# Expert cells of a two-block layer: who makes the low parts of the finished output tiles

## The reference, cut to what matters

```
he = jax.nn.silu(t @ exp_w1[e]) * (t @ exp_w3[e])      # 1024 -> 256
y  = y + comb[:, e:e + 1] * (he @ exp_w2[e])           # 256 -> 1024
```

## Time and profile before

| | |
|---|---|
| time, median of 3 runs | 2053.93 us (2053.76 to 2054.52) |
| span of the profiled execution, first to last instruction | 2052.0 us |
| TensorE busy | 1980.4 us, 97% |
| VectorE busy | 1415.1 us, 69% |
| ScalarE busy | 968.7 us, 47% |
| GpSimd busy | 24.6 us, 1% |
| mean granted TensorE clock | 0.988 |

### The profile page before, as it was taken

How to read it: one execution, slowest core, us unless ns; L and a number is a source line. 1 busy time by engine, 2 the same in 40 slices (tenths; PEclk the granted TensorE clock), 3 DMA queues, 4 the chain that set the end, 5 groups by cost and what they waited for, 6 DMA issues and landing times.

```text
span 2052.0 us, 26626 instructions
## 1 busy us (share of the span) xinstructions
PE 1980.4 (97%) x8972; PEld 1565.2 (76%) x8972; DVE 1415.1 (69%) x2180; ACT 968.7 (47%) x1409; POOL 24.6 (1%) x46
## 2 busy tenths in 40 slices
PE   7999999989999999899999999999998999999997
PEld 7887888877776778666667888888875678888885
DVE  7985443557999775857756888873387578888533
ACT  5666333446777335366654433333365454333221
POOL 0000000001000000000000000000000000000000
PEclk9999999999999999999999999999999999999998
DMA  4220322327999145300002233333341033332332
GB/s 182 79 67 20 94 92 92 98 77 262 356 353 340 62 113 161 106 1 1 2 1 90 88 99 92 92 102 103 103 119 41 12 102 98 96 92 92 103 103 82
DMA packets 65418, 219.09 MB, mean 107 GB/s; under 512 B 9584, under 2 KB 10768, under 8 KB 65200
## 3 DMA queue, kind: packets, MB, share of 16 engines
q1 hardware_dynamic: 60192, 211.04, 31.6%
q10 hardware_dynamic: 5136, 6.89, 1.4%
HBM read 209.04 MB, written 2.10 MB: 103 GB/s over the span
## 4 chain that ended last, share of the span: by engine, by line
PE 80%; DVE 11%; ACT 3%; issue 3%; DMA 1%; ACTq 1%; SPq 0%; DVEq 0%
PE psum L946 56%; PE psum L1370 5%; PE psum L1541 3%; PE psum L1296 2%; PE psum L1343 1%; PE psum L1677 1%; DVE w_lo L2645 1%; PE psum L1524 1%; PE psum L1353 1%; PE psum L1522 1%; PE psum L1110 1%; DVE sig L2892 1%; PE psum L1477 1%; PE psum L1538 1%; ACTq L1898 1%
## 5 line engine op out<-in xcount | busy, mean ns | idle before, releaser
L946 PE MATMUL psum<-x_hi,w_hi 128*128 128x512 f32 (+1 forms) x1344 | 497.8, 381 | 2.5 <-DVE w_lo L2645 1.4
L946 PE MATMUL psum<-x_lo,w_hi 128*128 128x512 f32 (+1 forms) x1344 | 497.7, 381 | 0.0
L946 PE MATMUL psum<-x_hi,w_lo 128*128 128x512 f32 (+1 forms) x1344 | 495.2, 379 | 0.0
L2645 DVE TENSOR_TENSOR w_lo<-raw,w_hi 128x1024 fp32r<-128x1024 f32 x243 | 296.5, 1220 | 188.7 <-ACT w_hi L1783 188.2
L1783 ACT ACTIVATE w_hi<-raw 128x1024 fp32r<-128x1024 f32 x243 | 255.6, 1054 | 208.0 <-DMA raw<-stream 205.5
L946 PEld LDWEIGHTS psum<-x_hi,w_hi 128*128 128x128 f32 x1344 | 246.7, 188 | 58.0 <-DVE w_lo L2645 2.8
L946 PEld LDWEIGHTS psum<-x_lo,w_hi 128*128 128x128 f32 x1344 | 246.4, 188 | 51.6 <-issue 1.4
L946 PEld LDWEIGHTS psum<-x_hi,w_lo 128*128 128x128 f32 x1344 | 247.0, 188 | 49.7
L946 PE MATMUL psum<-hid_hi,w_hi 128*128 128x512 f32 (+1 forms) x688 | 259.7, 385 | 11.8 <-DVE w_lo L2645 11.3
L946 PE MATMUL psum<-hid_lo,w_hi 128*128 128x512 f32 (+1 forms) x688 | 258.6, 384 | 0.0
L946 PE MATMUL psum<-hid_hi,w_lo 128*128 128x512 f32 (+1 forms) x688 | 257.9, 383 | 0.0
(11 more groups left out here) (611 smaller groups left out, 2996.5 us busy)
## 6 DMA issues: line engine op xcount, KB each, us to landing
raw<-stream SPq DMA_DIRECT2D x251, 512.0 KB, 3.6
raw<-experts SPq DMA_DIRECT2D x70, 512.0 KB, 5.3
raw_more<-experts SPq DMA_DIRECT2D x68, 512.0 KB, 5.3
staged<-staged ACTq DMA_DIRECT2D x80, 64.0 KB, 3.2
resid<-x_fm SPq DMA_DIRECT2D x4, 528.0 KB, 6.9
out_fm<-resid SPq DMA_DIRECT2D x4, 512.0 KB, 2.9
consts<-consts_in SPq DMA_DIRECT2D x1, 1373.0 KB, 13.0
kv_pairs<-kv_even_odd ACTq DMA_DIRECT2D x4, 256.0 KB, 7.4
```

The costliest lines, as they stand in the source:

```text
L946: last = pe.matmul(o, wt[:, slot, k * P:(k + 1) * P], m[part], start=start and p == 0, stop=stop and p == 2, skip_group_check=True)
L2645: dve.tensor_tensor(w_lo[:, slot, :], raw[:, slot, :], w_hi[:, slot, :].bitcast(F32), ALU.subtract)\
```

## The change

The low part of tiles 0 to 5 of `Y` moves from VectorE's queue to GpSimd's. GpSimd issues the six subtractions after it has set `Y` to zero, each behind a wait for the high part. VectorE keeps those of tiles 6 and 7, and before that of tile 6 waits until the six others are done.

```diff
@@ gpsimd
             for k in range(TILES):
                 pool.memset(Y[:, k, :], 0.0).then_inc(y_zeroed, 1)
 
+            for k in range(TILES - 2):
+                pool.wait_ge(y_hi, k + 1)
+                pool.tensor_tensor(YL[:, k, :], Y[:, k, :], YH[:, k, :].bitcast(F32), ALU.subtract).then_inc(y_lo, 1)
+
             pool.wait_ge(lin_done, L0["scat"] + C)
@@ vector
             def output_lo(k):
 
                 dve.wait_ge(y_hi, k + 1)
+                if k == TILES - 2:
+
+                    dve.wait_ge(y_lo, k)
                 dve.tensor_tensor(YL[:, k, :], Y[:, k, :], YH[:, k, :].bitcast(F32), ALU.subtract).then_inc(y_lo, 1)
@@ vector, loop over the cells
                 hidden_gate(c)
                 if c:
                     moe_low(6 * c + 6)
-                if c >= N_EXP + 1:
-                    output_lo(c - N_EXP - 1)
```

## The result

The changed kernel takes 2060.4 us, median of 7 runs (2058.9 to 2061.28), against 2053.93 us before: a ratio of 1.0031, 95% interval 1.0021 to 1.0041. It is slower by a little more than the 0.2% named in the prediction. Six other runs of the same kernel gave 2059.97 and 1.0032 (1.0020 to 1.0045). The profiled execution has a span of 2057.8 us, 5.8 above, and a time of 2059.58 us.

A forecast was written before the change was run, and what follows sets the result against it. VectorE was taken to bound late cells 17 to 21, TensorE the earlier ones. Cells 4.3, earlier stall 0.3 and tables 0.4 us summed to 5.0 us more, from 2053.93 to 2058.9 us; range 2050.2 to 2062.0.

The forecast's parts named there:

- What bounds: Late cells 17 to 21 go at VectorE's pace, 9.67 us against TensorE's 8.86; at most 3.6 us to win.
- the five cells: Cells 17 to 21, from 624.55 to 672.42: 47.87 us now, 44.30 at TensorE's pace.
- The duration of a subtraction: GpSimd's two-input subtraction of 1024 elements, D: taken as 2.3 us, bounds 1.0 and 2.7.
- The stop: GpSimd's subtraction blocks VectorE's `moe_low(6c+6)`, 2.0 us late; cell 10.53 us, 4.3 us over five cells; chance 0.6.
- The 96 ns of one cast: L914's first GpSimd cast, beside VectorE's L2645, took 706 ns against 610 undisturbed; read as one waiting for the other.
- the place of the stall: Stall lies one `moe_low` earlier than the removed instruction did, delaying a unit TensorE needs sooner: 0.3 us, once.
- The tail: Cell 22: the tables wait for GpSimd's sixth subtraction, starting at 677.7 instead of 677.31; 0.4 us more.
- Side by side: Rival: GpSimd and VectorE run together in the cells, TensorE bounds again, 3.6 us come back, 2050.4; chance 0.22.
- A quick GpSimd: Rival: GpSimd stops VectorE in the cells but D is below 1.4 us, a little won; D below 2.1 has 0.16.
- VectorE keeping the inputs from one instruction to the next: Rival: GpSimd gets in only at `output_add` (2054.1) or L3175 (2059.4); chance 0.08, half each.
- Slowed in part: Rival: in the cells both engines slow and neither stops; VectorE's cell 9.53 us, -0.7 us, 2053.2; chance 0.1.
- The clock is no part of this: TensorE's clock was granted at 1.00, the upper level of 2.4 GHz, in both windows of the cells.

The follow-up runs named there:

- the one-input kernel: Changed kernel with GpSimd's six subtractions replaced by copies of the same tile onto itself with one input; 2052.22 us, ratio 0.9996.

## Why the prediction was right, point by point

**What bounds.** Right. With memsets in place of GpSimd's subtractions the five cells took 44.33 us; 44.30 were named. The whole stretch fell by 3.0 and not by 3.6 us, since 0.6 were lost again at the tables.

**The duration of a subtraction.** Taken as 2.3 us between bounds of 1.0 and 2.7; it is 2.39 to 2.45. The lower bound was the case of one pass, and a copy with one input took 1.05. From 1.30 us for 512 columns to 2.40 for 1024 an element costs 2.15 ns, 2.6 times the casts' 0.83. The Trainium skill's figure in "GPSIMD Engine Reference", section "Performance versus the Vector engine", halved to 2.25 us as an estimate, was a little short of the 2.40 measured.

**The stop.** Right, and the forecast's core. The 96 ns of one cast were the only sign of it in the trace of before, and were the mechanism. The stall was computed as 2.0 us and is 1.98, by two small errors that cancel: the subtraction is 0.1 us longer, and VectorE goes on about 0.14 us before GpSimd's record ends. The pace of 10.53 us was met exactly, as was 4.6 for the five cells and the place of the stall (4.55). The Trainium skill, "SBUF — State Buffer", section "Who interferes with whom" (at "The single rule"), says that two SBUF inputs on VectorE contend with a GpSimd instruction that reads and not with one that only writes; 3.20 us for one `moe_low` beside the subtraction and 2.35 for two beside the memsets agree. Its statement that the second one is blocked in full agrees too, but for those last 0.14 us.

**The tail.** Mis-sized: 0.4 us was said, 0.1 measured. The tables were issued 4.87 us behind the last of the TensorE outputs above (at 681.61), as before (4.89), and the first took 607 ns for 474. The step that failed is small: GpSimd got the inputs some 0.14 us before the end of `moe_low`'s record, and VectorE got them back as much before the end of GpSimd's; the prediction let each wait for the whole record of the other.

**The rivals.** Side by side is out by the 3.20 us record. A quick GpSimd, below 1.4 us, is out by the 2.40. VectorE keeping the inputs from one instruction to the next is out by the first cast of the one-input kernel, which got in between two `moe_low` without a gap. Slowed in part is out: an instruction beside a reading GpSimd is longer by what was left of GpSimd's. (By its own parts the chances add up to 0.06, 0.46 and 0.48; it gives 0.07, 0.45 and 0.48.)

**What the sum left out.** 5.0 us were forecast and 4.7 to 4.9 measured in the stretch. The median rose by 6.5, since the stages behind, which were not touched, took 1.3 to 2.5 us longer; TensorE's clock was at its lower level for longer there. "The clock is no part of this" was read in the windows of the cells, where it holds; I did not ask what a shift does to the later gaps. The time of 2060.4 lies within the range, 1.5 above the forecast, for a reason that the prediction did not have.

## What to carry to other kernels

Moving an instruction from a saturated VectorE to an idle GpSimd paid here only where GpSimd's instruction did not read SBUF while VectorE's next one needed two inputs from it; otherwise the price was nearly what was left of GpSimd's duration, 1.98 us for 1.14 saved. If it must read, give it a piece about as long as a VectorE instruction with an input in PSUM, and let it wait from one instruction earlier, so that it begins with that one; half a tile beside `output_add` turned 4.7 us lost in the stretch into 2.4 won. And a stopped instruction shows as a longer record, so compare durations by form before and after, not only idle time.

## What the runs showed of the hardware that was not expected

A table with one input in SBUF and the result in SBUF, 128x512 in 0.47 us, is stopped by a reading GpSimd as well: 2597 ns in one case, 607 in another.

GpSimd, waiting while `moe_low` ran, started as that ended and ahead of the next `moe_low`, although VectorE's queue had no gap (a cast of 1.05 us with 0.86 us of waiting before it, and 0.84 us more for the next `moe_low`).

TensorE's low-clock stretch behind one and the same gap lasted 13.7 us in six profiles and 17.1 us in eight; which of the two an execution gets is not explained by the runs.
